# Query projection of a hybrid decoder step: one product of 512 prompt columns and one of 32 sampled columns per weight tile, instead of two of 272

## The reference, cut to what matters

```python
D_MODEL, SEQ, DEC_BATCH, DEC_SEQ, NSA_WIDTH = 1024, 512, 8, 4, 512
n = modulate(rmsnorm(x, norm_g[l, 1]), shift[:, 1], scale[:, 1])
qa, kva, ga, qb, fb, ib, gb, ma, mb = jnp.split(n @ w_in[l], splits, axis=-1)
...
logits = jnp.einsum('bqgrd,bkgd->bgrqk', qg, k, preferred_element_type=jnp.float32) * NSA_SCALE
```

## Time and profile before

| | us |
|---|---|
| median of 3 runs (3233.45 to 3238.41) | 3235.15 |
| span of the profiled execution | 3240.8 |
| PE busy in it | 3004.2 (93%) |
| PEld busy | 2850.6 (88%) |
| DVE busy | 1343.8 (41%) |
| ACT busy | 967.6 (30%) |

### The profile page before, as it was taken

The page is one execution under the profiler, slowest core; times in us unless marked ns, Lnnn a source line. Parts: engine busy times, 40 slices in busy tenths (PEclk is TensorE's granted clock), DMA queues, the critical chain, the costliest instruction groups (busy, mean ns, idle before and its releaser), DMA issues. The chain is left out here.

```text
span 3240.8 us, 58790 instructions
## 1 busy us (share of the span) xinstructions
PE 3004.2 (93%) x24911; PEld 2850.6 (88%) x24911; DVE 1343.8 (41%) x2788; ACT 967.6 (30%) x1593; POOL 57.4 (2%) x32
## 2 busy tenths in 40 slices
PE   6999998889779898999989999888995998899998
PEld 4999998778569898999989999887883998899998
DVE  3332334356455453333352333443663735423334
ACT  2222222344342233222232222332443313322222
POOL 0000000000030000000000000000000200000000
PEclk7999998999889898999999999999997989899999
DMA  6746224441342335332246433263215425222322
GB/s 210 242 135 202 86 83 147 108 130 53 105 125 80 112 114 195 105 91 85 85 160 218 143 100 91 78 176 124 73 40 162 103 61 157 71 86 86 91 85 74
DMA packets 524375, 378.65 MB, mean 117 GB/s; under 512 B 43186, under 2 KB 469576, under 8 KB 522803
## 3 DMA queue, kind: packets, MB, share of 16 engines
q1 hardware_dynamic: 493620, 307.30, 32.9%
q10 hardware_dynamic: 30496, 67.64, 5.7%
HBM read 344.10 MB, written 39.07 MB: 118 GB/s over the span
## 5 line engine op out<-in xcount | busy, mean ns | idle before, releaser
L192 DVE TENSOR_TENSOR w_lo<-w_raw,w_hi 128x1024 fp32r<-128x1024 f32 (+1 forms) x390 | 481.3, 1234 | 1098.6 <-ACT w_hi L187 1098.4
L187 ACT ACTIVATE w_hi<-w_raw 128x1024 fp32r<-128x1024 f32 (+1 forms) x390 | 405.7, 1041 | 1316.2 <-PE pa L204 681.9
L204 PE MATMUL pa<-nhi,w_hi 128*128 128x272 f32 x1408 | 297.1, 292 | 28.7 <-DVE nlo L247 26.8
L204 PE MATMUL pa<-nhi,w_lo 128*128 128x272 f32 x1408 | 293.7, 290 | 0.0
L204 PE MATMUL pa<-nlo,w_hi 128*128 128x272 f32 x1408 | 292.9, 290 | 0.0
L204 PE MATMUL pa<-ghi,w_hi 128*128 128x272 f32 x1408 | 291.6, 288 | 1.3 <-DVE glo L794 1.3
L204 PE MATMUL pg<-nhi,w_lo 128*128 128x272 f32 x1408 | 292.8, 290 | 0.0
L204 PE MATMUL pg<-nhi,w_hi 128*128 128x272 f32 x1408 | 292.7, 289 | 0.0
L204 PE MATMUL pg<-nlo,w_hi 128*128 128x272 f32 x1408 | 291.9, 289 | 0.0
L204 PE MATMUL pa<-ghi,w_lo 128*128 128x272 f32 x1408 | 291.0, 288 | 0.0
L204 PE MATMUL pa<-glo,w_hi 128*128 128x272 f32 x1408 | 290.3, 288 | 0.0
(11 more groups left out here) (352 smaller groups left out, 4588.7 us busy)
## 6 DMA issues: line engine op xcount, KB each, us to landing
w_raw<-in_ffn_w_in SPq DMA_DIRECT2D x352, 192.0 KB, 2.8
ada_raw<-in_ada_w ACTq DMA_DIRECT2D x26, 2048.0 KB, 9.7
w_raw<-in_w_in SPq DMA_DIRECT2D x156, 192.0 KB, 2.9
w_raw<-in_ffn_w_out SPq DMA_DIRECT2D x128, 192.0 KB, 2.7
w_raw<-in_ffn_w_in SPq DMA_DIRECT2D x176, 128.0 KB, 2.9
ada_raw<-in_ada_w SPq DMA_DIRECT2D x10, 2048.0 KB, 15.1
w_raw<-in_ffn_w_out SPq DMA_DIRECT2D x160, 128.0 KB, 2.5
w_raw<-in_w_in SPq DMA_DIRECT2D x94, 128.0 KB, 3.0
```

The lines of the kernel that those rows point to most:

```text
L187: act.activation(self.hi[slot][:, 0:k, :], self.raw[slot][:, 0:k, :], ACT.Copy).then_inc(self.hi_done, 1)
L192: dve.tensor_tensor(self.lo[slot][:, 0:k, :], self.raw[slot][:, 0:k, :], self.hi[slot][:, 0:k, :].bitcast(F32), ALU.subtract).then_inc(sel ...
L204: mm = pe.matmul(out[:, half, 0:HALF], w[slot][:, k0 + n, :], x[:, n, half * HALF:(half + 1) * HALF], start=(n == 0 and w is self.hi and x ...
```

## The change

Only the query tiles of `rows_stage` change. Instead of calling the helper, the loop is written out, with the same three terms for each chunk; the two pieces of a term are the 512 prompt columns, into bank 0, and the 32 sampled columns, into the first 32 columns of bank 1. The copy out of `pq` reads both banks as one row of 1024 columns and takes its first 544, in one piece.

```diff
-                        mm = wt.some(pe, slot, pq, nhi, nlo, DC, 4 * second, 4 * second + 4)
+                        for k in range(4 * second, 4 * second + 4):
+                            for w, v, end in ((wt.hi, nhi, False), (wt.hi, nlo, False), (wt.lo, nhi, True)):
+                                for bank, t0, t1 in ((0, 0, SEQ), (1, SEQ, T)):
+                                    mm = pe.matmul(pq[:, bank, 0:t1 - t0], w[slot][:, k, :], v[:, k, t0:t1],
+                                                   start=(k == 0 and w is wt.hi and v is nhi), stop=(k == DC - 1 and end))
                         if second:
                             mm.then_inc(wt.mm_done, 1)
...
-                        dve.tensor_scalar(pj[:, Q0 + i, :].rearrange("p (h t) -> p h t", h=2), pq[:, :, 0:HALF],
+                        dve.tensor_scalar(pj[:, Q0 + i, :], pq[:, :, :].rearrange("p h t -> p (h t)")[:, 0:T],
                                           DH ** -0.5, None, ALU.mult).then_inc(ev_done, 1)
```

## The result

The changed kernel takes 3250.54 us (median of 5 runs, 3247.24 to 3251.81). The kernel before, measured beside it, takes 3238.41 us (5 runs, 3233.45 to 3241.85). The ratio is 1.0033, with a 95% interval of 1.0019 to 1.0047: slower by some 10.7 us. The time lies 1.5 us above the stated range, and the direction is the one that was forecast. Two later measurements of the same pair gave 1.0041 (1.0025 to 1.0056) and 1.0031 (1.0020 to 1.0042).

What follows compares the result with a forecast made beforehand. TensorE, busy 93% of the span, was taken to bound the kernel. Pairs growing 0.086 us, less waits taken up, add 8.5 us to 3235.15, giving 3243.7 us, with a stated range of 3234 to 3249.

Steps and rivals of the forecast that it cites:

- the base: Whole kernel before the change: unprofiled median 3235.15 us, taken as 5.7 us below the profiled span of 3240.8.
- the sum: Rounds of both layers: 4.7 us more in one and 3.8 in the other, together 8.5 us (6.8 to 10.4).
- The wide matmul: 512-column product in the rounds: 0.216, 0.225 or 0.235 us, taken as 0.225, with the next load hidden under it.
- The load: After each 32-column product in the rounds, loading the next product's weights is not hidden and takes 0.111 us.
- The end of a round: A round's last pair is followed by a transpose with a shorter load, leaving 0.05 us less uncovered.
- The round without waits: Before the change a round takes 3.94 us, or 4.14 where it waits for the copy out of PSUM.
- One load ahead, and no further: On TensorE, the loader loads the next matmul's weights while one runs, then stands idle, for 0.05 us in the trace.
- no change: Rival, chance 0.17: loads in the rounds could begin earlier, so a pair stays at 0.250 us and the kernel at 3235.
- All waits taken up: In the rounds, the slower TensorE absorbs all 7.2 us of waits, 3.2 and 4.1 us in the two layers.
- The waits stay: Rival, chance 0.04: chains behind the rounds' waits move with TensorE, nothing is absorbed, 15.8 us more, 3251 us.
- Doubled narrow matmuls: Rival, chance 0.05: each 32-column product in the rounds runs with two loads, another 0.111 us per pair, 3265 us.
- The clock: Rival, chance 0.04: the granted clock falls in the rounds, 4.4 us more in each layer, 3252 us.

Runs made afterwards that it cites:

- 480 and 64: The changed kernel with each pair of products cut at 480 and 64 columns instead of 512 and 32, copied out in two pieces; 3253.52 us, one run.
- third after: The changed kernel, unchanged, measured a third time against the kernel before; 3249.7 us (11 runs), ratio 1.0031.
- control: The kernel before, unchanged under another name, measured against itself; 3241.01 us (12 runs) to 3236.91 (23 runs), ratio 1.0012.
- lone 512 columns: The changed kernel without its 32-column products, so only the 512-column ones remain; 3240.17 us, one run.
- lighter weights: The changed kernel with weights of 32 columns instead of 128 for the 512-column products, except a tile's first and last; 3240.9 us, one run.
- 352 and 192 columns: The changed kernel with each pair cut at 352 and 192 columns instead of 512 and 32, copied out in two pieces; 3238.42 us, one run.
- narrow products twice: The changed kernel with each 32-column product issued two times; 3271.25 us (4 runs), ratio to the kernel before 1.0113.

## Why the prediction was right or wrong

**The step that failed is the base.** "The span of the profiled execution, 3240.8, becomes 3249.3; the median without profile lies 5.7 us lower" took the median of three runs for what before takes, and 5.7 us for what the profile adds. The profile adds nothing of that kind: profiled executions of after, 480 and 64, and the third after had times 1.7 to 1.8 us above their spans (3247.24 to 3245.5, 3253.52 to 3251.7, 3252.95 to 3251.2). A span of 3240.8 goes with a run of about 3242.5; the profiled execution of before was one of its longer ones, and the three runs were short ones. Later medians of before are 3238.41, 3235.11, 3236.91 and 3239.32 us, and single runs lie between 3230.5 and 3248.0. The range's "2 us of spread on either side" was too narrow for that. Of the 6.9 us between 3243.65 and 3250.54, the base is 3.3, the sum 0.5, and 3.1 stay open (below). From 3238.41, the median measured beside after, the same sum gives 3246.9, and the range of 3234 to 3249, moved up by as much, would have held the measured time. A median of three says where before lies to some 3 us, and the range should have had that on both sides. The record shows what most of this spread goes with: of the 63 runs of before and its control, nine at a mean granted clock of 0.949 took 3243.3 us in the mean, twenty at 0.951 took 3238.5 and ten at 0.953 took 3235.9 (the clock is the mean of the whole execution).

**The sum was near: 9.0 us in the rounds, forecast 8.5.** Small terms were off and partly cancelled.

- *The wide matmul*: 0.234 us, taken as 0.225. It is the upper of the three bounds, the one in which the surplus goes by the column. The choice "from the row of the same operand type" had the right row and the wrong form: the 0.012 us over 272 columns is 0.457 ns a column, not a sum for each matmul. The 480, 352 and lone 512 columns show it.
- *The load* behind the narrow product: 0.1085, forecast 0.111. The pair is 0.343 instead of 0.336.
- *The end of a round*: the 0.05 us saved at the transposes is there. Loads of after, for the first two transposes behind the last narrow product of round 0:

```profile
584.60 0.14 PEld L1087 LDWEIGHTS pt<-ident,cn 128*128 128x128 f32 x1
584.66 0.14 PEld L1087 LDWEIGHTS pt<-ident,cn 128*128 128x128 f32 x1
```

The step is 0.06 us instead of 0.1085.
- *The round without waits*: 3.94 us was read from round 0, which itself begins behind a wait. Its eight transposes are shown with 1.09 us, those of rounds that begin without one with 1.03, so that such a round took 3.88. Twelve pairs at 0.093 more, less the 0.05, are 1.07 us, and after takes 4.94 (614.97 to 619.91), 1.06 more. One round of 4.97, four of 4.94 and three of 5.17 are 40.24, and 40.26 and 40.23 were measured.

**One load ahead, and no further: right.** In the query tiles of after no load begins less than 0.1 us after the one before it, the pair is 0.343 us, and with lighter weights it falls to 0.263. The rival "no change" falls by this. One sign of it did not come as it was worded: between the starts of matmuls there are 0.316 us from wide to narrow and 0.027 from narrow to wide, not 0.225 and 0.111, and a wide row begins 0.084 us ahead of the load that was to begin with it. The forecast steps are found between loads (0.234 and 0.1085). The loader's idle time of 0.05 us was read from shown durations: loads shown with 0.19 us follow each other 0.1085 apart, so it idles longer than that. The rule of the Trainium skill ("TensorE: Matmul & The Clock Gate", Back-to-back issue gap) from which it also followed, with prices by moving columns alone, isn't borne out for this operand type: 0.234 us for 512 columns by themselves instead of 0.216, and 0.343 for a pair instead of 0.241. The same section of the Trainium skill gives these prices for an isolated product and says that in a stream of loads and products both set the spacing; the prediction left that out, and the pairs bear it out. The 25 ns that it states for short products come close to the 0.027 us from a narrow row to the next.

**All waits taken up: right.** The rounds of after have no wait in either layer, and both layers come to the same 40.2 us though they waited 3.2 and 4.1 before by the forecast's count. "The waits stay" gave 3251, the nearest of all to the measured 3250.54, and is wrong: by it the rounds would have taken 43.2 and 44.1 us. With a base 3 us too low, a right sum missed and a wrong one hit; only the stretch tells them apart. **"Doubled narrow matmuls"** falls by the pair (0.343, and 0.457 with a second narrow product). **The clock** stayed at 1.00 in the rounds of all three profiles of after; it fell in the last rounds of the control, and in the first rounds of one layer with 352 and 192 columns (0.66) and with the narrow products twice (0.74).

**SP, ACT and DVE as cover, and the copy out of PSUM: right.** The last rows went out as early as before. DVE's scaling takes 0.72 us in one run of columns (L1152), as it did in two (L1148).

**What stays open.** The rounds give 9.0 us, a ratio of 1.0028, which lies in all three intervals (1.0033, 1.0041, 1.0031); their mean, 1.0035, is 11 us. Whether the 2 us between are real isn't settled. The mean granted clock does not account for them: runs of after at 0.949, 0.951 and 0.953 (3, 6 and 4 of them) took 3255.5, 3249.3 and 3246.5 us in the mean, 12.2, 10.9 and 10.6 more than those of before and its control at the same clock. The stretches outside the rounds differ between profiles of one kernel by more than these 2 us, and the control differed from its own twin by 1.0012.

## What to carry to other kernels

A product hides the next weight load only if its moving columns last as long as the load: cut 544 columns into pieces that are all long enough, not into one that fills a bank and a rest. Where a stage has waits with a pace of their own, a cost or a gain shows there only net of them, so read the stage's end and not the instruction. Take the base of a forecast from as many runs as there are, and give it its own share of the range.

## What the runs showed of the hardware

- A column of this operand type costs 0.457 ns at the full clock (512 columns in 0.234 us) and 0.83 at the half clock (272 in 0.225): twice the clock gives 1.8 times the pace.
- The load of 128 weight columns of this type takes 0.1085 us (that of a transpose 0.06) and runs beside the moving columns of the product before it; the longer of the two sets the step. Behind 32, 64 and 192 moving columns the step is 0.1085, behind 272 and more the load is not seen. With a load of 32 weight columns the step behind a narrow product is 0.028, which may be that load or the narrow product's own least time (0.027 between the matmuls' rows in after).
- A matmul's row can begin before its load is over (by 0.084 us for the wide ones of after), so where a load isn't hidden, the distance between two matmul rows is not the price of the first. The sum over a repeating group, and the starts of loads, are safe to read.
- The granted clock fell in the control's last rounds, behind waits of 1.9 us for cached rows, and not in the first profile of before behind waits as long. One full profile of a stretch at 1.00 doesn't say that it always runs there.
